# Attention layers' ends: scores between tiles, transposes by pairs, a norm of four chunks

## The chip, the cores and the metric

One core of a Trainium2 chip runs the whole program in one launch. The metric is device microseconds of that core, the median of several runs; a smaller number is better.

## The reference, cut to what matters

The program is a chain of seven stages on a sequence of 256 rows of width 1024: a gated feed-forward, a mixing stage, a second gated feed-forward, and then the second block, on which the change bears. That block has two layers, each an attention followed by a feed-forward with squared ReLU, and after each half a layer norm:

```
h = x * (1.0 + scale1) + shift1
y = moba_attention(h, ...)   # layer 0: 16 heads of 64, causal softmax
y = diff_attention(h, ...)   # layer 1: 8 heads, softmax(q1 k1) - lam * softmax(q2 k2)
x = layer_norm(ALPHA * x + (1.0 + gate1) * y, g, b)
h = x * (1.0 + scale2) + shift2
y = sq_relu_mlp(h, ...)
x = layer_norm(ALPHA * x + (1.0 + gate2) * y, g, b)
```

With 256 rows MoBA's only block is its own, so its attention is plain causal attention. In diff_attention each head's output also passes an RMS norm over its 128 columns. Both end in a product with a 1024x1024 output matrix.

## The kernel before, in words

Five engines run programs of their own, written out in order and tied by semaphores: SP loads weights, ACT and DVE split them and do the elementwise work, PE multiplies, POOL loads small tables. Each engine takes its instructions strictly in this written order, so the place of a wait matters as much as the wait.

**Weights.** Every product is made in fp32 accuracy from three products: hi x hi, hi x lo, lo x hi (`three`, L449 to L451). A unit is 128x2048 weights (1 MB) in one of six ring slots. ACT writes its high part (`split_hi`, L913), DVE the low part (`split_lo`, L1263), four units ahead of PE (`AHEAD`). An attention layer has 16 units: 0 to 11 are q, k and v (six blocks of two units), 12 to 15 the output matrix. For one unit PE makes 24 matmuls of 512 columns: two tiles t (128 rows each) x four chunks k x three products. Units 12 and 13 take chunks 0 to 3 of the attention's output, units 14 and 15 chunks 4 to 7. Unit 12 and 14 make columns 0 to 511 of the result, 13 and 15 the rest.

**A chunk of attention.** There are eight chunks c of 128 columns (two heads in MoBA, one head with two softmaxes in the other). For each, five steps pass between the engines; the table `ATTENTION` sets in which slot (behind which unit, or between its tiles) PE issues each:
- S: PE makes scores in banks 0 and 1 (`scores`, L809, L811), DVE scales, masks and finds the maxima (`scores` of DVE, L1778), ACT the exponentials (`exps`, L1194). In the second layer DVE then mixes the two softmaxes (`combine`, L1789 to L1795).
- W: PE transposes the weights into bank 2 (`weights_T`, L826), ACT copies them (`weights_out`, L1183).
- O: PE multiplies with v (`outputs`, L838 to L841) into the second half of bank 3. DVE divides by the sums (L1824, L1826); in the second layer ACT first takes squares (`squares`, L1204), and DVE multiplies by the gain (L1814) and later by the norm's factor (`norms`, L1804, then ten small steps in L1292 to L1301, then L1808).
- T: PE transposes finished output chunks (`outputs_T`, L559), ACT writes their high part (`chunk_his`, L920), DVE the low part (`chunk_los`, L1272). These feed units 12 to 15.
- H (L559, L1766): transposes of q and k heads, once per half.

ACT and DVE walk the same table and do the work of a slot's events one slot later. `probs` (the scores and exponentials of a chunk) is one buffer, `top` too; `total` has two. So scores(c) on DVE waits for the transposes of chunk c-1. In the table of before, T0 stands for all four chunks 0 to 3 behind unit 11, and T1 for chunks 4 to 7 behind O7; behind unit 13 come S7, O5, W6, O6, W7, O7 and T1 with no unit between them. In the second layer the norm is taken over chunks 0 to 2, then 3, then 4 to 6, then 7.

**The layer's end.** The layer norm (`after_ln`) works on four quarters of the result (tile t, half n): DVE adds the residual and takes statistics (`ln_part`, L1367 to L1370), for tile 0 both halves, then some nine small steps, then ACT normalises (L944), PE transposes (L523), ACT and DVE scale and split (L936, L1283, L1284), and the feed-forward's first unit can start.

Of the kernel before, what the change touches and what calls it, by code (L numbers as in the profile page):

```python
# [98 lines left out]
def quarter_buffer(b, t, h):  # L99
# [9 lines left out]

ATTENTION = [(0, [], []), (1, [], []), (2, [], []), (3, [], ["H0"]), (4, [], ["H1"]), (5, [], ["S0"]),  # L110
# [32 lines left out]
def two_blocks_kernel(nc, d, out):  # L143
    with ExitStack() as ctx:
# [50 lines left out]
        top = sb("top", [P, 2, NT])  # L195
        total = sb("total", [P, 2, 4])
# [9 lines left out]
        def part(off, n, t=None):  # L206
# [31 lines left out]
        probs = part(10240, 768)  # L238
        probs_w = part(11008, 384)
        rope2_t = [part(11392 + 128 * i, 128, NT) for i in range(4)]  # L240
        probsT = part(11904, 768)
        causal = part(12672, 3 * P)
        rot2 = part(13056, 4 * 8 * ROT).rearrange("p (c t n) -> p c t n", c=2, t=NT)
# [48 lines left out]
            sem(n) for n in ("rel_zero", "rel_in", "rel_out", "bias_in", "bias_done"))  # L292
        at_s, at_m, at_e, at_w, at_t, at_p, at_sq, at_o, at_out = (
# [152 lines left out]
        def _(pe):  # L446
# [345 lines left out]
            def attention(s, u0, pb, hb, ab, ch_o, diff):  # L792
# [22 lines left out]
                def weights_T(c):  # L815
# [5 lines left out]
                    if c % 4 == 0:  # L821
                        pe.wait_ge(at_out, ab + c)
                    src, n = (probs_w, 3) if diff else (probs, 6)
# [5 lines left out]
                def outputs(c):  # L829
# [3 lines left out]
                    n_e, width = (1, 2 * HD) if diff else (2, HD)  # L833
                    for e in range(n_e):
# [10 lines left out]
                def outputs_T(half):  # L845
                    pe.wait_ge(at_out, ab + 4 * half + 4)
                    if half == 0:
# [3 lines left out]
                    chunks_of(o2, half * BANK, 4, 4 * BANK if half == 0 else 0)  # L851
# [11 lines left out]

                entry(u0, s, zt if diff else x)
                do = {"H": heads_T, "S": scores, "W": weights_T, "O": outputs, "T": outputs_T}
                for slot, between, events in ATTENTION:
                    if slot is not None and 3 <= slot < 12:
                        if not between:
                            proj(u0, pb, slot // 2, slot % 2)
                        else:  # L870
# [1159 lines left out]
```

## Time and profile before

| | |
|---|---|
| median of 3 runs | 1284.71 us (1284.48 to 1284.99) |
| profiled execution | 1284.9 us, span 1283.1 us |
| PE busy | 1230.5 us (96%), 5777 matmuls |
| DVE, ACT, POOL busy | 931.4 (73%), 609.5 (48%), 95.7 us (7%) |
| MoBA layer's unit 11 to the first matmul of the feed-forward behind it | 706.82 to 762.33 us |
| the same of the second layer | 1027.15 to 1087.71 us |

The profiled execution's own time is 1.8 us over its span. The span runs from the first to the last instruction, all positions below are counted from its start. PE's rows carry modelled ends: a matmul of 512 columns starts 0.23 us after the one before it and is shown with 0.39 us. PEclk is the granted TensorE clock, 1.00 for 2.4 GHz and 0.50 for 1.2 GHz.

### The profile page before, as it was taken

The page shows a single profiled execution, that of the slowest core. Times are in us where ns is not written, and L with a number is a line of the kernel's source. Part 1 is how long each engine was busy: PE and PEld are TensorE (multiplying, and loading weights), DVE is VectorE, ACT ScalarE, POOL GpSimd, SP SyncE. Part 2 cuts the span into 40 slices and gives each one's busy share as a digit, 9 for nine tenths or more (in the row PEclk, how much of TensorE's full clock was granted, in tenths as well). Part 3 has the DMA queues.
Part 4 walks back from the last instruction along what each step waited for, and adds up shares of the span by engine and source line. Part 5 has one row for each costly group of instructions (what it writes and reads, how often), then busy time and mean ns, then how long its engine had stood idle before and what let it go on. Part 6 is the DMA issues. An engine that isn't in the chain of part 4 may idle for free.

```text
span 1283.1 us, 14651 instructions
## 1 busy us (share of the span) xinstructions
PE 1230.5 (96%) x5777; PEld 1010.8 (79%) x5777; DVE 931.4 (73%) x1349; ACT 609.5 (48%) x801; POOL 95.7 (7%) x136
## 2 busy tenths in 40 slices
PE   7999999999999999999999989999999986999996
PEld 6888887888888878888788768888877764888885
DVE  6789868865556698888775458896878776755446
ACT  6344446545664454443555535443455552634340
POOL 2100221003400010000000000000000000000000
PEclk9999999999999999999999979999999997999998
DMA  9999985544454598997473436798635441465530
GB/s 301 336 327 325 315 266 205 171 158 156 156 165 166 179 348 317 308 311 256 142 259 119 132 131 233 259 328 283 257 132 197 182 131 66 160 206 208 194 133 33
DMA packets 132916, 274.31 MB, mean 214 GB/s; under 512 B 6240, under 2 KB 51504, under 8 KB 132848
## 3 DMA queue, kind: packets, MB, share of 16 engines
q1 hardware_dynamic: 114992, 209.80, 47.6%
q0 software_dynamic: 17792, 63.56, 14.4%
q8 instruction: 46, 0.75, 0.2%
q14 instruction: 22, 0.18, 0.0%
q10 hardware_dynamic: 64, 0.02, 0.0%
HBM read 270.41 MB, written 2.93 MB: 213 GB/s over the span
## 4 chain that ended last, share of the span: by engine, by line
PE 87%; DVE 8%; ACT 2%; issue 2%; DMA 1%; ACTq 0%; DVEq 0%
PE ps L449 26%; PE ps L451 26%; PE ps L450 26%; PE ps L559 3%; DVE lo_w L1263 2%; ACT hi_w L913 1%; DMA w_raw<-in_diff_w_in 1%; PE ps L523 1%; PE ps L699 1%; PE ps L826 1%; PE ps L686 1%; PE ps L723 1%; PE ps L811 0%; PE ps L809 0%; PE ps L838 0%
## 5 line engine op out<-in xcount | busy, mean ns | idle before, releaser
L1263 DVE TENSOR_TENSOR lo_w<-w_raw,hi_w 128x2048 fp32r<-128x2048 f32 x197 | 447.3, 2290 | 99.1 <-ACT hi_w L913 98.9
L449 PE MATMUL ps<-hi_w,xT_hi 128*128 128x512 f32 x1120 | 449.7, 402 | 11.9 <-DVE xT_lo L1284 7.4
L451 PE MATMUL ps<-lo_w,xT_hi 128*128 128x512 f32 x1120 | 440.3, 393 | 0.0
L450 PE MATMUL ps<-hi_w,xT_lo 128*128 128x512 f32 x1120 | 439.6, 393 | 0.0
L913 ACT ACTIVATE hi_w<-w_raw 128x2048 fp32r<-128x2048 f32 x197 | 372.9, 1916 | 43.6 <-DMA w_raw<-in_w_mix_out 11.8
L449 PEld LDWEIGHTS ps<-hi_w,xT_hi 128*128 128x128 f32 x1120 | 212.8, 190 | 59.5 <-issue 15.7
L451 PEld LDWEIGHTS ps<-lo_w,xT_hi 128*128 128x128 f32 x1120 | 212.4, 190 | 46.0
L450 PEld LDWEIGHTS ps<-hi_w,xT_lo 128*128 128x128 f32 x1120 | 212.8, 190 | 42.0
L449 PE MATMUL ps<-hi_w,hT_hi 128*128 128x512 f32 x464 | 181.9, 392 | 0.4 <-DVE hT_lo L1426 0.4
L451 PE MATMUL ps<-lo_w,hT_hi 128*128 128x512 f32 x464 | 180.7, 389 | 0.0
L450 PE MATMUL ps<-hi_w,hT_lo 128*128 128x512 f32 x464 | 180.5, 389 | 0.0
L1426 DVE TENSOR_TENSOR hT_lo<-ps,hT_hi 128x512 fp32r<-128x512 f32 (+1 forms) x38 | 34.7, 914 | 93.6 <-ACT hT_hi L1046 67.4
L449 PEld LDWEIGHTS ps<-hi_w,hT_hi 128*128 128x128 f32 x464 | 87.1, 188 | 18.6 <-DVE hT_lo L1426 0.9
L451 PEld LDWEIGHTS ps<-lo_w,hT_hi 128*128 128x128 f32 x464 | 87.1, 188 | 18.2
L450 PEld LDWEIGHTS ps<-hi_w,hT_lo 128*128 128x128 f32 x464 | 87.2, 188 | 17.8
L1442 DVE SCALAR_TENSOR_TENSOR piece_acc<-aux,c_act,piece_acc 128x512 f32<-128x512 f32 x119 | 89.3, 751 | 3.6
L1046 ACT ACTIVATE hT_hi<-ps 128x1024 fp32r<-128x1024 f32 x16 | 16.4, 1027 | 131.4 <-PE ps L559 131.4
L1009 ACT ACTIVATE hT_hi<-ps 128x512 fp32r<-128x512 f32 x22 | 13.2, 598 | 114.0 <-PE ps L559 114.0
L559 PE MATMUL ps<-ident,area 128*128 128x128 f32 x384 | 53.5, 279 | 11.1 <-DVE area L1808 7.7
L559 PEld LDWEIGHTS ps<-ident,area 128*128 128x128 f32 x384 | 46.2, 143 | 20.6 <-DVE area L1808 8.4
L1001 ACT ACTIVATE area<-ps,rstd_x 128x256 f32<-128x256 f32 x44 | 18.5, 472 | 57.5 <-PE ps L451 57.5
L1902 POOL DMA_DIRECT2D aux<-in_ada_w x34 | 25.6, 753 | 234.4 <-DVE piece_acc L1442 213.4
(221 smaller groups left out, 887.9 us busy)
## 6 DMA issues: line engine op xcount, KB each, us to landing
w_raw<-in_ffn_w_in SPq DMA_DIRECT2D x86, 512.0 KB
aux<-in_ada_w POOLq DMA_DIRECT2D x34, 1024.0 KB, 6.4
w_raw<-in_mlp_w_up SPq DMA_DIRECT2D x32, 1024.0 KB
w_raw<-in_mlp_w_down SPq DMA_DIRECT2D x32, 1024.0 KB
w_raw<-in_w_mix_in SPq DMA_DIRECT2D x26, 1024.0 KB
w_raw<-in_ffn_w_out SPq DMA_DIRECT2D x22, 1024.0 KB
area<-in_ada_w POOLq DMA_DIRECT2D x14, 1024.0 KB, 7.5
w_raw<-in_moba_w_in SPq DMA_DIRECT2D x12, 1024.0 KB
```

The source lines that it names most:

```text
L449: pe.matmul(dst, lhs_hi, rhs_hi, start=start, stop=False)
L450: pe.matmul(dst, lhs_lo, rhs_hi, start=False, stop=False)
L451: return pe.matmul(dst, lhs_hi, rhs_lo, start=False, stop=stop)
L559: mm = pe.transpose(ps[:, off:off + P], src[:, t, col0 + c * P:col0 + (c + 1) * P], ident[:, :])
L913: act.activation(hi_w[:, ring_slot(u), :], w_raw[:, ring_slot(u), :], ACT.Copy).then_inc(w_hi, 1)
L1001: ins = act.activation(act_s[:, t, 0:FF_B], ps[:, (pair + t) * BANK:(pair + t) * BANK + FF_B], ACT.Silu, scale=rstd_x[:, t:t + 1])
L1009: act.activation(hi[:, c0:c0 + 2, :], ps[:, off:off + 2 * SEQ].rearrange("p (c n) -> p c n", c=2), ACT.Copy).then_inc(hidT_hi, 1)
L1046: act.activation(hi[:, c0:c0 + 4, :], bank(pair, 2).rearrange("p (c n) -> p c n", c=4), ACT.Copy).then_inc(hidT_hi, 1)
L1263: vec.tensor_tensor(lo_w[:, ring_slot(u), :], w_raw[:, ring_slot(u), :], hi_w[:, ring_slot(u), :].bitcast(F32), ALU.subtract).then_inc(w_l ...
L1426: vec.tensor_tensor(lo[:, c0:c0 + chunks, :], src.rearrange("p (c n) -> p c n", c=chunks), hi[:, c0:c0 + chunks, :].bitcast(F32), ALU.subt ...
L1442: ins = vec.scalar_tensor_tensor(out=acc, in0=row, scalar=c_act[:, c:c + 1], in1=acc, op0=ALU.mult, op1=ALU.add)
L1902: pool.dma_start(dst, ada[layer][:, 4 * half:4 * half + 4, i * BANK:(i + 1) * BANK])\
```

## The change

The table is rewritten from unit 11 on, and slot 13 differs by layer:

```diff
-             (9, ["H2"], ["O2", "W3"]), (10, ["H3"], ["S4", "O3"]), (11, [], ["T0", "S5", "W4"]),
-             (12, [], ["S6", "O4", "W5"]), (13, [], ["S7", "O5", "W6"]), (None, [], ["O6", "W7"]),
-             (None, [], ["O7"]), (None, [], ["T1"]), (14, [], []), (15, [], [])]
+             (9, ["H2"], ["O2", "W3"]), (10, ["H3"], ["S4", "O3"]), (11, ["S5", "T0"], ["T1", "W4"]),
+             (12, ["S6"], ["O4", "W5"])]
+MOBA_SLOTS = ATTENTION + [(13, ["S7", "O5", "W6"], ["O6"]), (14, [], [])]
+DIFF_SLOTS = ATTENTION + [(13, ["S7"], ["O5", "W6", "O6"]), (14, [], [])]
+PAIR_BANK, NORMED = (4, 5, 0, 1), (1, 2, 3, 3)
```

The middle list of a slot is issued between the unit's two tiles. T0 to T3 are now pairs of chunks, each in a bank of its own. `probs` and `top` have two buffers, `total` four:

```diff
-        probs = part(10240, 768)
-        probs_w = part(11008, 384)
+        probs = [part(10240, 768), part(11008, 768)]
+        moba_probsT = part(11776, 768)
+        probs_w, diff_probsT = part(11776, 384), part(12160, 384)
...
-                    if c % 4 == 0:
+                    if c % 4 == 0 or c == 7 and not diff:
                         pe.wait_ge(at_out, ab + c)
...
+                        if not diff:
+                            outputs_T(2)
+                        weights_T(7)
+                        outputs(7)
+                        if diff:
+                            outputs_T(2)
+                            outputs_T(3)
+                        pe.wait_ge(w_lo, u0 + 15)
+                        last_quarter(0, 0, 0)
+                        if not diff:
+                            outputs_T(3)
+                        pe.wait_ge(w_lo, u0 + 16)
+                        last_quarter(1, 0, 0)
+                        last_quarter(0, 0, 2).then_inc(part_done, 1)
+                        last_quarter(1, 0, 2).then_inc(part_done, 1)
```

`last_quarter(n, t, c)` makes the six matmuls of unit 14+n, tile t, for two chunks; for tile 0 it takes chunks 4 and 5 of both units first, then 6 and 7 of both. Tile 1 follows as before. On DVE:

```diff
                     vec.wait_ge(at_s, ab + c + 1)
-                    vec.wait_ge(at_e, ab + c)
-                    if diff:
-                        vec.wait_ge(at_w, c)
-                    else:
-                        vec.wait_ge(at_t, ab + c)
+                    if c >= 1:
+                        vec.wait_ge(at_e, ab + c - 1)
+                    if diff and c >= 2:
+                        vec.wait_ge(at_w, c - 1)
+                    elif not diff and c >= 2:
+                        vec.wait_ge(at_t, ab + c - 1)
...
-                        if c % 4 < 3:
+                        if c % 4 < 3 and c < 6:
                             vec.wait_ge(at_p, ab + c + 2)
...
+                    if diff and slot == 10:
+                        norms(0, 2)
+                    if diff and slot == 11:
+                        norms(2, 2)
...
+                if diff:
+                    outputs(5)
+                    combine(7)
+                    outputs(6)
+                    outputs(7)
+                    norms(4, 4)
+                    pair_los(2)
+                else:
+                    outputs(6)
+                    pair_los(2)
+                    outputs(7)
+                pair_los(3)
+                split_lo(u0 + 18)
```

and on ACT, behind the last slot:

```diff
+                if diff:
+                    squares(6)
+                    weights_out(7)
+                    squares(7)
+                    pair_his(2)
+                else:
+                    pair_his(2)
+                    weights_out(7)
+                pair_his(3)
+                split_hi(u0 + 18)
```

Before, `split_hi(u0 + 18)` and `split_lo(u0 + 18)` stood behind O6's work and ahead of chunk 7's. The exponentials' wait is now for the chunk four back.

PE at the end of the MoBA layer before, from O7 to unit 14's first matmuls (L838 to L841 are O7, L559 is T1, L449 to L451 unit 14):

```order
L838 MATMUL ps<-area 128x64 [waits proj_out,at_outputs_out,at_weightsT_out]
L839 MATMUL ps<-area 128x64
L841 MATMUL ps<-area 128x64
...
L559 MATMUL ps<-ident,area 128x128 [waits at_max,at_outputs_out]
L559 MATMUL ps<-ident,area 128x128 x7
L449 MATMUL ps<-hi_w,xT_hi 128x512 [waits ch_lo,w_lo]
```

and now, from behind O6 (L564 are the pairs T2 and T3, L831 is W7, L844 starts O7, L454 unit 14 and then unit 15):

```order
L564 MATMUL ps<-ident,area 128x128 [waits at_max,at_outputs_out]
L564 MATMUL ps<-ident,area 128x128 x3
L831 MATMUL ps<-ident,area 128x128 [waits at_outputs_out,at_weightsT_out,at_exp]
L831 MATMUL ps<-ident,area 128x128 x5
L844 MATMUL ps<-area 128x64 [waits proj_out,at_outputs_out,at_weightsT_out]
...
L454 MATMUL ps<-hi_w,xT_hi 128x512 [waits ch_lo,w_lo]
...
L564 MATMUL ps<-ident,area 128x128 [waits at_max,at_outputs_out]
L564 MATMUL ps<-ident,area 128x128 x3
L454 MATMUL ps<-hi_w,xT_hi 128x512 [waits ch_lo,w_lo]
```

T2 has moved ahead of W7, and T3 stands between the first six matmuls of unit 14 and those of unit 15.

DVE at the same place before (L1824 and L1826 are outputs 6, then 7; L1263 splits unit 18; L1272 is the low part of chunks 4 to 7; L1367 opens the layer norm):

```order
L1824 RECIPROCAL inv<-total 128x4 [waits at_weightsT_out,at_outputs]
L1826 TENSOR_TENSOR area<-ps,inv 128x2x2x64 [waits vec_step]
L1263 TENSOR_TENSOR lo_w<-w_raw,hi_w 128x2048 [waits w_hi]
L1824 RECIPROCAL inv<-total 128x4 [waits at_outputs]
L1826 TENSOR_TENSOR area<-ps,inv 128x2x2x64 [waits vec_step]
L1272 TENSOR_TENSOR xT_lo<-ps,xT_hi 128x256 [waits ch_act] x4
L1367 TENSOR_TENSOR area<-ps,aux 128x512 [waits ld_row,part_done]
```

and now (L1886 and L1888 outputs, L1334 low parts by pairs, L1325 the split, L1429 the layer norm):

```order
L1886 RECIPROCAL inv<-total 128x4 [waits at_outputs]
L1888 TENSOR_TENSOR area<-ps,inv 128x2x2x64 [waits vec_step]
L1334 TENSOR_TENSOR xT_lo<-ps,xT_hi 128x256 [waits ch_act] x2
L1886 RECIPROCAL inv<-total 128x4 [waits at_outputs]
L1888 TENSOR_TENSOR area<-ps,inv 128x2x2x64 [waits vec_step]
L1334 TENSOR_TENSOR xT_lo<-ps,xT_hi 128x256 [waits ch_act] x2
L1325 TENSOR_TENSOR lo_w<-w_raw,hi_w 128x2048 [waits w_hi]
L1429 TENSOR_TENSOR area<-ps,aux 128x512 [waits ld_row,part_done]
```

The split of unit 18 has moved from ahead of outputs 7 to a place right ahead of the layer norm, and outputs 6 no longer waits for the copy of W7 (at_weightsT_out).

DVE in the second layer, around unit 12's start before (L1795 ends combine(4), L1263 splits unit 15, L1272 is the low part of chunks 0 to 3, L1778 scores 5):

```order
L1795 SCALAR_TENSOR_TENSOR area<-area,inv 128x256
L1263 TENSOR_TENSOR lo_w<-w_raw,hi_w 128x2048 [waits w_hi]
L1272 TENSOR_TENSOR xT_lo<-ps,xT_hi 128x256 [waits ch_act] x4
L1778 ISA area,top<-ps,area 128x128 [waits at_weights,at_exp,at_scores]
```

and now (L1334 low parts, L1852 to L1858 combine(4), L1841 scores 5, L1325 the split):

```order
L1334 TENSOR_TENSOR xT_lo<-ps,xT_hi 128x256 [waits ch_act] x2
L1852 SCALAR_TENSOR_TENSOR head_eps<-total 128x2 [waits at_weightsT,at_exp]
...
L1858 SCALAR_TENSOR_TENSOR area<-area,inv 128x256
L1841 ISA area,top<-ps,area 128x128 [waits at_weights,at_exp,at_scores]
...
L1325 TENSOR_TENSOR lo_w<-w_raw,hi_w 128x2048 [waits w_hi]
L1334 TENSOR_TENSOR xT_lo<-ps,xT_hi 128x256 [waits ch_act] x2
```

The first pair of low parts comes ahead of combine, scores and the split, the second pair behind all three.

## Rows read from the trace of the kernel before

**Rows 1.** PE's waits, 620 to 765 us: line <- releaser: us in total, times, longest.

```profile
PE ps L449 <- DVE xT_lo L1284: 2.9, 2, 2.2
PE ps L838 <- issue: 2.0, 1, 2.0
PE ps L838 <- ACT area L1183: 1.7, 1, 1.7
PE ps L559 <- DVE area L1826: 1.1, 1, 1.1
PE ps L826 <- ACT area L1194: 0.7, 1, 0.7
PE ps L449 <- DVE xT_lo L1272: 0.4, 1, 0.4
```

**Rows 2.** The same, 930 to 1095 us.

```profile
PE ps L559 <- DVE area L1808: 7.7, 2, 6.8
PE ps L838 <- issue: 3.2, 2, 1.6
PE ps L449 <- DVE xT_lo L1272: 2.8, 2, 2.3
PE ps L826 <- DVE area L1795: 1.6, 1, 1.6
```

**Rows 3.** Windows of PE: stretch, length, busy (instructions), PEclk, DMA share, GB/s.

```profile
706.82:762.33 55.51, 47.20 (x243) 0.88 0.30 105
1027.15:1087.71 60.56, 43.05 (x208) 0.86 0.29 97
1040.00:1042.00 2.00, 2.00 (x6) 0.50 0.00 0
978.00:982.00 4.00, 2.51 (x12) 1.00 0.19 51
```

**Rows 4.** The chain of waits in order of time: start, us, what.

```profile
748.28 0.43 PE ps L450
...
770.77 0.23 PE ps L450
...
1060.49 0.63 ACT aux L1204 x4
```

**Rows 5.** ACT's groups, 700 to 765 us: busy us, mean ns | idle before.

```profile
L913 ACT ACTIVATE hi_w<-w_raw 128x2048 fp32r<-128x2048 f32 x5 | 9.5, 1901 | 0.0
...
L1183 ACT ACTIVATE area<-ps 128x768 f32<-128x768 f32 x4 | 3.2, 812 | 8.3 <-PE ps L826 8.3
...
L920 ACT ACTIVATE xT_hi<-ps 128x256 fp32r<-128x256 f32 x8 | 2.5, 384 | 6.8 <-PE ps L559 6.8
```

**Rows 6.** DVE's groups, the same stretch.

```profile
L1263 DVE TENSOR_TENSOR lo_w<-w_raw,hi_w 128x2048 fp32r<-128x2048 f32 x5 | 11.4, 2290 | 11.5 <-ACT hi_w L913 11.5
L1778 DVE CUSTOM_DVE_ANT_0 area<-ps,area 128x256 f32<-128x256 f32 x8 | 3.4, 420 | 0.0
...
L1826 DVE TENSOR_TENSOR area<-ps,inv 128x256 f32<-128x256 f32 x5 | 2.1, 424 | 0.2
```

**Rows 7.** DVE's timeline: start, us, instruction.

```profile
750.86 0.69 DVE L1367 TENSOR_TENSOR area<-ps,aux 128x512 f32<-128x512 f32 x1 [3.58 <-PE ps L451]
...
753.58 0.69 DVE L1367 TENSOR_TENSOR area<-ps,aux 128x512 f32<-128x512 f32 x1 [0.57 <-PE ps L451]
...
757.72 0.16 DVE L1382 SCALAR_TENSOR_TENSOR shift<-moments,rstd 128x1 f32<-128x1 f32 x1
...
1051.18 0.75 DVE L1795 SCALAR_TENSOR_TENSOR area<-area,inv 128x128 f32<-128x128 f32 x2
...
1061.60 0.17 DVE L1804 TENSOR_TENSOR head_sq<-head_sq,head_eps 128x6 f32<-128x6 f32 x1
...
1063.82 0.96 DVE L1808 TENSOR_TENSOR area<-area,head_rstd 128x768 f32<-128x768 f32 x1
...
1069.65 0.43 DVE L1808 TENSOR_TENSOR area<-area,head_rstd 128x256 f32<-128x256 f32 x1
```

More of the change, by code:

```diff
@@ L850, in outputs_T @@
                         pe.wait_ge(at_m, ab + 8)
-                    chunks_of(o2, half * BANK, 4, 4 * BANK if half == 0 else 0)
+                    chunks_of(o2, 2 * pair * P, 2, PAIR_BANK[pair] * BANK)
                 def modulation_rows():
@@ L862, in modulation_rows_2, with last_quarter @@
                         .then_inc(mod_T, 1)
+                def last_quarter(n, t, c):
+                    u = u0 + 14 + n
+                    rhi = hi_w[:, ring_slot(u), :].rearrange("p (k n) -> p k n", k=4)
+                    rlo = lo_w[:, ring_slot(u), :].rearrange("p (k n) -> p k n", k=4)
+                    for k in range(c, c + 2):
+                        if t == 0:
+                            pe.wait_ge(ch_lo, ch_o + 4 + k + 1)
+                        mm = three(bank(4 + n + 2 * t), xT_hi[:, 4 + k, tile(t)], xT_lo[:, 4 + k, tile(t)],
+                                   rhi[:, k, :], rlo[:, k, :], False, k == 3)
+                    return mm
@@ L1840, in attention @@
                             scores(int(event[1:]))
+                    for event in last_between:
+                        if event[0] == "S" and diff:
+                            combine(int(event[1:]))
                     for event in before:
@@ L1853, in attention @@
                             combine(int(event[1:]))
-                    if diff and ("O2" in before or "O6" in before):
-                        c = 2 if "O2" in before else 6
-                        vec.wait_ge(at_out, ab + c + 1)
-                        then(norms(c - 2, 3))
-                    if slot is not None and slot < 14:
-                        split_lo(u0 + slot + AHEAD)
+                    for event in between:
+                        if event[0] == "S":
+                            scores(int(event[1:]))
+                    split_lo(u0 + slot + AHEAD)
                     if slot == 2 and diff:
@@ L1864, in attention @@
                         second_modulation()
-                    if "O7" in events:
-                        split_lo(u0 + 18)
-                    before = events
+                    for event in between:
+                        if event[0] == "O":
+                            outputs(int(event[1:]))
+                    before, last_between = events, between
+                if diff:
+                    outputs(5)
[4 more added lines that the diff above has]
+                    pair_los(2)
+                else:
+                    outputs(6)
[3 more added lines that the diff above has]
+                split_lo(u0 + 18)
             attention(U_MOBA, PB_MOBA, 4, NA_H, CH_MOBA_O, False)
```

157 lines of the change are left out of this document (90 added, 67 removed).

## The prediction

> **What bounds the kernel now.** The page first: PE is busy 96% of the span, so only PE's holes and the stretches in which its clock is low can be won. The edits bear on the last units of the two attention layers, so I read PE's waits there. In the MoBA layer they are short and many [rows 1]: 2.0 us of "issue" at an outputs step (O6), 0.7 at W7, 1.7 at O7, 1.1 at T1, 0.4 at unit 14, and 2.2 at the feed-forward's first unit. With 0.2 that the first tile of unit 12 waits, the stretch from unit 11 to the feed-forward has 8.4 us of shown holes. In the second layer [rows 2] it is 6.8 behind DVE's norm at T1 and 0.9 at T0, 2.3 and 0.5 at units 12 and 14, 3.2 at O6 and O7, 1.6 at W7, and again 2.2 at the feed-forward: 17.5 us. The windows of both stretches [rows 3] give their lengths, 55.5 and 60.6 us, and that the granted clock was 0.88 and 0.86 there. A matmul at the lower level, 1.2 GHz, goes on after 0.43 us and one at 2.4 GHz after 0.23 [rows 4], so each costs 0.20 more.
>
> From this comes what PE must work in each stretch. A hole as shown leaves out the modelled tail of the matmul before it, about 0.2 to 0.25 us (0.39 shown, 0.23 to the next); seven such holes are 1.7 us in the MoBA layer, eight are 2.0 in the other. Clock: in the MoBA layer I count W7, O7, T1 and some eight matmuls of unit 14 at the lower level, 4.3 us lost; in the second layer seven matmuls of unit 12 (the window at 1040 is at 0.50 [rows 3]), O7, T1 and two or three of unit 14, 3.4 us. Work at full clock is then 55.5 - 8.4 - 1.7 - 4.3 = 41.1 us, and 60.6 - 17.5 - 2.0 - 3.4 = 37.7 us. The change alters no PE work (120 large matmuls, three scores, four weights and outputs, the sixteen transposes of T stay), so what counts is the new holes. I count these whole, with their tails.
>
> **The change, part by part: MoBA layer.** Scores between the tiles: S5, S6 and S7 are 2.7 us (twelve matmuls of 0.23) earlier, and the exponentials with them. O6 now stands behind tile 1 of unit 13 and finds outputs 5 and the copy of W6 ready: its 2.0 us hole goes. At W7 PE now waits for outputs 6: O6's tail of 0.2 and the two steps of DVE (0.2, and 0.42 for L1826 [rows 6]), of which T2's four transposes, about half a us, hide most: 0.4 us. O7 waits for W7's copy: 0.81 [rows 5] and tail and handshake of 0.35, 1.2 us; nothing hides it, and it is cheaper than before only because outputs 6 no longer follows that copy. T2's high and low parts are done by then. T3 waits for outputs 7, made beneath the six matmuls of unit 14 (1.4 us), and its copies lie under the six of unit 15: no hole. The second pair at unit 12 is late by 0.2 us, since DVE splits unit 15 ahead of it. Unit 12's first tile no longer waits for the last projection.
>
> Then the end pays. Take T3's first transpose as zero. ACT's copy is done at 1.4 (0.7 for the four transposes, 0.7 for two L920 of 384 ns, less overlap), and only then splits unit 18's high part, 1.90 us [rows 5], and DVE the low part, 2.29 [rows 6]: DVE is free at about 5.5. All of it stood earlier before. The first quarter of the layer norm is ready on PE at 3.5, so it starts 2.0 us late. From 753.58 to the shift's end at 757.88 is 4.3 us, and the quarter ahead of it takes 2.2 (750.86 to the statistics' end, [rows 7]): 12.0. With 0.8 for ACT's normalising the transposes can start at 12.9. PE has its own work done at 10.3 (0.5 of transposes, then 6 + 12 + 24 matmuls). Hole: 2.5 us, where there was 0.1. Interleaving the units by chunks makes it worse: quarter (0, 0) comes only 1.4 us ahead of (0, 1), and DVE needs 2.2 for it, so of the 2.5 about 0.8 would stand without the split. With 0.3 between the two transposes and 2.3 to the first unit as before, the holes are 0.2 + 0.4 + 1.2 + 2.5 + 0.3 + 2.3 = 6.9 us, plus 0.4 for the clock at these transposes. After: 41.1 + 6.9 + 0.4 = 48.4 against 55.5: 7.1 us less. Neither hole at W7 or O7 should drop the clock: 1.5 us in one piece at 980 left it at 1.00 [rows 3].
>
> **Second layer.** DVE is the tight engine. norms(2, 2) stands ahead of combine(4): ten small steps and L1804 take 2.2 us whatever the width (1061.60 to 1063.82), and the multiply 0.96 for 768 columns and 0.43 for 256 [rows 7], so about 0.7 for 512. Scores 4 end after norms(0, 2) and a split, which leaves 0.6 at S5, and combine(4), 1.3 us (0.75 for its last two steps at 1051.18 [rows 7], 0.5 for the three small ones), another 0.6 at W4. From the first pair's low part DVE goes on to combine, scores (four passes of 0.42 or less [rows 6], 1.2 together), the split of 2.3 and only then the second pair, 0.3: 5.0 us. PE has 0.2 left, T1, the 0.6, W4 and six matmuls, 3.0: hole 2.0. So here 3.2 us replace the 3.2 of before, nothing is won, and 1.5 us of lower clock behind them stays.
>
> Behind unit 13 S7 and combine(7) are ahead of time. O6 waits for W6's copy, 1.1; W7 for combine(7), 0.5; O7 for a copy of 0.5, 0.85 in all. T2 waits for the squares, 0.63 [rows 4], L1814, 0.4, and one norm of four chunks, 2.2 + 1.2 = 3.45: with the tail 4.9 us. Before, the same point was 6.8 late since norm 4 to 6, the split of unit 18 (2.3) and a second norm of 2.6 stood in line. The first of unit 14 waits 1.0 for copy and low part. Here T2 and T3 come together ahead of all 48 matmuls, so the split of unit 18 is over in time and only the interleaving costs: 0.65. Sum: 0.6 + 0.6 + 2.0 + 1.1 + 0.5 + 0.85 + 4.9 + 1.0 + 0.65 + 0.3 + 2.3 = 14.8 us. Clock: 1.5 at unit 12, 1.1 at T2, T3 and unit 14, 0.3 at the end: 2.9. After: 37.7 + 14.8 + 2.9 = 55.4 against 60.6: 5.2 us less.
>
> Costs I put at nothing: two score buffers in slots 5 to 10, since PE has no hole there but those at the head transposes; moved areas; the wait of W7 for outputs 6 beyond what is counted. The last split hides behind the layer norm in one layer only. The feed-forward starts behind the same 2.2 us hole as before, so it keeps the same stretch at 1.2 GHz. Weight loads are no closer: their DMA share in both stretches is 0.3 [rows 3]. Each hole rests on one handshake that I know to 0.1 us, and there are seventeen; together with the clock, known to 1.5 us a layer, the sum of 12.3 us lies between 9 and 16.
>
> **Sum.** 1284.9 (the profiled execution) - 12.3 = 1272.6; the median of the runs shown is 0.2 lower, so 1272.4 us.
>
> **The rivals.**
> First: DVE in the second layer. Between units 10 and 13 it gets a norm, both splits, combine and scores in one line with PE waiting behind each; if any is later than I count, units 12 and 13 wait for it and the holes move rather than close. For it speaks that PE's longest waits there are all on DVE [rows 2]; against it that DVE's work is unchanged in sum, one norm less. It would win 2 instead of 5.2 in this layer: 1275.6.
>
> Second: the clock takes back part in the MoBA layer. Holes of 0.4 and 1.2 us stand 0.6 us apart, the ones at the end make 5.1 in 6 us. If the first pair brings it down, some 9 us at 1.2 GHz follow, ten to fifteen matmuls at 0.20 and the small steps: 2.5 us, 1274.9. Against: 980 us, above. The other way, if the 2.0 us hole at unit 12 of the second layer leaves the clock up, 1.5 more is won: 1270.9.
>
> Third, and this one ends slower: PE's many short holes hold the clock at 1.2 GHz from unit 12 to the end of both layers. Before, one long pause let PE run 40 to 48 matmuls in a piece at 2.4 GHz; now every group is cut. 96 large matmuls per layer at 0.20 are 19 us; for half of them in each layer, 19 us in all, the result is 1272.4 + 19 = 1291. It decides from about 60 matmuls at the lower level on (12.3 / 0.20). Against it: between the new holes stand 3 to 6 us of unbroken work. The Trainium skill states such a rule (TensorE: Matmul & The Clock Gate, section "A second HAM failure mode: psum-queue depth-cycling"): a kernel whose PE pauses shortly and often between groups of matmuls swung between both clock levels and lost throughput. By that rule this change, which spreads PE's groups, would come out at 1291; the trace has it only behind holes of 2 us and more.
>
> Fourth: the change does not do what it says, since each step still waits for the one before and only the place of the wait moves. Then both layers stay within 2 us of before: 1283.
>
> **How the numbers follow.** Forecast 0.62, with its own range 1269 to 1276; DVE's line 0.14 and the clock in the MoBA layer 0.13; held clock 0.03; nothing gained 0.04; anything else slower 0.01, anything else faster 0.03. The range that leaves two in ten out goes to 1268.5 below (the clock stays up at unit 12 and some holes are shorter) and to 1278 above (both first rivals together, with a part of the unknown). About 0.2%, 2.6 us, is what can be told from no change. Faster 0.92, same 0.04, slower 0.04.
>
> **What would show it.** In the profile after: no hole of over 0.3 us between unit 11 and O6 in the MoBA layer; 1.2 us at O7; the layer norm's first step right behind the split of unit 18 and a hole of 2 to 3 us ahead of the first transposes of the feed-forward, against under 1 in the second layer; there 4 to 6 us ahead of T2, behind a single norm of eight columns, and about 2 us within unit 12's first tile. Wrong would be: PEclk near 0.5 over unit 13 of the MoBA layer, a hole of over 3 us on weights, or an S step that waits for DVE by over 1 us.

## The result, and the profile after

The changed kernel takes 1269.8 us (median of 4 runs, 1269.74 to 1271.83) against 1284.6 before: a ratio of 0.9891 (0.9879 to 0.9903), 14.8 us less. Forecast were 1272.4 us, 12.3 less. The profiled execution has a span of 1268.0 us (before 1283.1) and a mean granted clock of 0.99 (before 0.982).

The two stretches that the change touches, as windows of the trace after; the columns are those of [rows 3]:

```profile
706.24:754.82 48.58, 43.13 (x243) 0.97 0.40 137
1019.52:1072.78 53.26, 41.44 (x208) 0.93 0.34 115
```

By the places of these windows the 15.1 us of span come from: the MoBA stretch 6.9 (55.51 to 48.58), the second layer's 7.3 (60.56 to 53.26), and 0.9 from the three parts around them (0.6, 0.1 and 0.2). Both clocks rose, from 0.88 to 0.97 and from 0.86 to 0.93.

PE's waits, 625 to 1095 us, answer to [rows 1] and [rows 2] together (us in total, times, longest):

```profile
PE ps L454 <- DVE xT_lo L1346: 5.8, 4, 2.2
PE ps L564 <- issue: 4.7, 1, 4.7
PE ps L528 <- ACT area L977: 4.5, 4, 2.3
PE ps L844 <- ACT area L1217: 2.4, 3, 0.9
PE ps L454 <- DVE xT_lo L1334: 2.1, 2, 1.7
...
PE ps L831 <- DVE area L1858: 0.5, 2, 0.3
PE ps L831 <- DVE area L1888: 0.4, 1, 0.4
PE ps L814 <- DVE top L1841: 0.3, 1, 0.3
```

The 2.0 us at O6 of the MoBA layer is gone, the 1.7 us at its O7 is down to 0.9, the three of 1.6 us in the second layer are down to 0.9, 0.2 and 0.6, and the 6.8 us behind DVE's norm to 4.7. The greatest that remain are this 4.7 us, one of 2.3 ahead of the MoBA layer's feed-forward transposes, the feed-forwards' own 2.2, and 1.7 at unit 12. Where each stands, in PE's timeline of the MoBA layer (start, us, instruction, idle time before it and its releaser):

```profile
733.96 0.85 PE L831 MATMUL ps<-ident,area 128*128 128x128 f32 x6 [0.38 <-DVE area L1888]
...
735.71 0.43 PE L844 MATMUL ps<-area 128*128 128x64 f32 x2 [0.90 <-ACT area L1217]
...
751.12 1.82 PE L528 MATMUL ps<-ident,area 128*128 128x128 f32 x8 [2.30 <-ACT area L977]
...
754.82 0.77 PE L454 MATMUL ps<-hi_w,xT_hi 128*128 128x512 f32 x1 [1.88 <-DVE xT_lo L1346]
```

and of the second layer:

```profile
1027.80 0.55 PE L831 MATMUL ps<-ident,area 128*128 128x128 f32 x3 [0.30 <-DVE area L1858]
...
1031.44 0.50 PE L454 MATMUL ps<-hi_w,xT_hi 128*128 128x512 f32 x1 [1.70 <-DVE xT_lo L1334]
...
1046.39 0.46 PE L844 MATMUL ps<-area 128*128 128x128 f32 x2 [0.89 <-ACT area L1217]
1047.53 0.55 PE L831 MATMUL ps<-ident,area 128*128 128x128 f32 x3 [0.23 <-DVE area L1858]
1048.65 0.49 PE L844 MATMUL ps<-area 128*128 128x128 f32 x2 [0.58 <-ACT area L1217]
1054.29 1.94 PE L564 MATMUL ps<-ident,area 128*128 128x128 f32 x8 [4.70 <-issue]
1056.68 0.77 PE L454 MATMUL ps<-hi_w,xT_hi 128*128 128x512 f32 x1 [0.45 <-DVE xT_lo L1334]
...
1069.24 1.36 PE L528 MATMUL ps<-ident,area 128*128 128x128 f32 x8 [0.49 <-ACT area L977]
1072.78 0.77 PE L454 MATMUL ps<-hi_w,xT_hi 128*128 128x512 f32 x1 [2.17 <-DVE xT_lo L1346]
```

DVE's timeline answers to [rows 7]. First the MoBA layer's end, then the second layer between the two low parts ahead of unit 12, then the norm of four chunks ahead of T2:

```profile
741.67 2.29 DVE L1325 TENSOR_TENSOR lo_w<-w_raw,hi_w 128x2048 fp32r<-128x2048 f32 x1 [1.04 <-ACT hi_w L946]
743.88 0.68 DVE L1429 TENSOR_TENSOR area<-ps,aux 128x512 f32<-128x512 f32 x1
...
1025.81 0.75 DVE L1334 TENSOR_TENSOR xT_lo<-ps,xT_hi 128x256 fp32r<-128x256 f32 x2
...
1028.77 2.29 DVE L1325 TENSOR_TENSOR lo_w<-w_raw,hi_w 128x2048 fp32r<-128x2048 f32 x1
1030.97 0.75 DVE L1334 TENSOR_TENSOR xT_lo<-ps,xT_hi 128x256 fp32r<-128x256 f32 x2
...
1050.74 0.17 DVE L1869 TENSOR_TENSOR head_sq<-head_sq,head_eps 128x8 f32<-128x8 f32 x1
...
1052.96 1.23 DVE L1873 TENSOR_TENSOR area<-area,head_rstd 128x1024 f32<-128x1024 f32 x1
```

The layer norm (L1429) starts in the very moment in which the split of unit 18 ends. The second low part ahead of unit 12 comes 5.16 us behind the first (forecast 5.0), behind combine, scores and a split. The norm is one line of 3.45 us (forecast 3.45), 1050.74 to 1054.19, and T2 follows at 1054.29.

The clock, in PE's windows after; [rows 3] had 0.50 at unit 12 of the second layer:

```profile
752.00:754.00 2.00, 0.94 (x4) 0.50 0.95 307
1030.00:1032.00 2.00, 0.56 (x2) 1.00 0.80 310
1032.00:1034.00 2.00, 2.00 (x14) 1.00 0.00 0
1052.00:1054.00 2.00, 0.00 (x0) 0.50 0.00 0
```

Behind the 1.70 us hole the clock now stays up. Read in such windows from 20 us to PE's last matmul, the time at 1.2 GHz fell from 37.5 us to 17.0 (behind that matmul, where PE has nothing left to do, both traces have one more low stretch up to their end): before 13.6 us from 736 on, 3.4 from 762, 3.4 from 1038, 13.7 from 1060 and 3.4 from 1086; after 6.8 from 750, 6.8 from 1050 and 3.4 from 1072.

### The profile page after: what moved, and what is told of

It is laid out like the page before. It is cut to its first block, busy times and chain, and to the rows that moved or that the text cites. A ratio compares the mean times of both kernels' runs of the same rounds, so it can differ in the third digit from the quotient of the medians.

```text
span 1268.0 us, 14635 instructions
## 1 busy us (share of the span) xinstructions
PE 1223.2 (96%) x5777; PEld 1003.9 (79%) x5777; DVE 928.9 (73%) x1337; ACT 609.2 (48%) x801; POOL 95.2 (8%) x136
## 4 chain that ended last, share of the span: by engine, by line
PE 83%; DVE 8%; ACT 3%; DMA 3%; issue 2%; SPq 1%; DVEq 0%; ACTq 0%
PE ps L454 25%; PE ps L456 25%; PE ps L455 25%; PE ps L564 3%; DVE lo_w L1325 2%; ACT hi_w L946 1%; DMA w_raw<-in_ffn_w_out 1%; DMA w_raw<-in_diff_w_in 1%; DMA w_raw<-in_ffn_w_in 1%; PE ps L528 1%; PE ps L704 1%; PE ps L831 1%; DVE area L1430 1%; DVE bst L1432 1%; DVE area L1429 1%
## 5 line engine op out<-in xcount | busy, mean ns | idle before, releaser
L1325 DVE TENSOR_TENSOR lo_w<-w_raw,hi_w 128x2048 fp32r<-128x2048 f32 x197 | 447.5, 2290 | 86.5 <-ACT hi_w L946 86.0
L454 PE MATMUL ps<-hi_w,xT_hi 128*128 128x512 f32 x1120 | 449.1, 401 | 10.3 <-DVE xT_lo L1346 7.1
L454 PEld LDWEIGHTS ps<-hi_w,xT_hi 128*128 128x128 f32 x1120 | 211.5, 189 | 59.0 <-issue 13.2
L454 PE MATMUL ps<-hi_w,hT_hi 128*128 128x512 f32 x464 | 182.0, 392 | 0.5 <-DVE hT_lo L1488 0.5
L454 PEld LDWEIGHTS ps<-hi_w,hT_hi 128*128 128x128 f32 x464 | 87.1, 188 | 18.7 <-DVE hT_lo L1488 0.9
L1042 ACT ACTIVATE hT_hi<-ps 128x512 fp32r<-128x512 f32 x22 | 13.1, 597 | 112.5 <-PE ps L564 112.5
L564 PE MATMUL ps<-ident,area 128*128 128x128 f32 x384 | 53.2, 277 | 7.8 <-issue 4.7
L564 PEld LDWEIGHTS ps<-ident,area 128*128 128x128 f32 x384 | 45.6, 142 | 17.8 <-issue 5.5
```

The source lines that it names most:

```text
L454: pe.matmul(dst, lhs_hi, rhs_hi, start=start, stop=False)
L564: mm = pe.transpose(ps[:, off:off + P], src[:, t, col0 + c * P:col0 + (c + 1) * P], ident[:, :])
L1042: act.activation(hi[:, c0:c0 + 2, :], ps[:, off:off + 2 * SEQ].rearrange("p (c n) -> p c n", c=2), ACT.Copy).then_inc(hidT_hi, 1)
L1325: vec.tensor_tensor(lo_w[:, ring_slot(u), :], w_raw[:, ring_slot(u), :], hi_w[:, ring_slot(u), :].bitcast(F32), ALU.subtract).then_inc(w_l ...
```

## The experiments

The main theory: the holes close as forecast, each for its own reason, and what the sum missed is clock. The rivals: DVE's line in the second layer, clock taken back in the MoBA layer, and a gain that comes from somewhere else, such as the buffers.

**Each layer alone.** A copy of before's program of an attention layer stands beside the new one, for one layer.

```diff
-            attention(U_DIFF, PB_DIFF, 8, NA_H + 8, CH_DIFF_O, True)
+            attention_old(U_DIFF, PB_DIFF, 8, NA_H + 8, CH_DIFF_O, True)
```

> The new order and the new waits in the MoBA layer alone; the second layer keeps the old table, norms and end. Theory (the gain is the sum of holes closed in each layer, and the layers don't touch each other): the stretch from unit 11 to the feed-forward is 48.6 us in the MoBA layer and 60.6 in the second, 7 us off the whole: 1277.6. Rival (part of the gain of one layer is lost or made in the other, by loads or by the clock): this run and the one with the second layer alone don't add up to 14.8 within 1 us.

Measured: 1278.9 us (1277.9 to 1279.3), ratio 0.9957 (0.9940 to 0.9973), 5.6 us less. The stretch in the MoBA layer is 48.4 us (expected 48.6). The hole ahead of the feed-forward's transposes is 2.33 us, and in the second layer both great holes of before stand: 2.33 us at unit 12 and 6.84 at T1.

> The new order in the second layer alone. Theory: 55.5 us in the MoBA layer and 53.3 in the second, 7.3 us off the whole: 1277.3; PEclk stays at 1.00 through units 12 and 13 of the second layer. Rival (the clock stayed up there only because the whole program had moved against it): the clock falls within unit 12 as before, and 5.8 us are won, as I had predicted for this layer with its clock: 1278.8.

Measured: 1277.0 us (1276.3 to 1277.5), ratio 0.9942 (0.9927 to 0.9957), 7.5 us less. Unit 12's hole is 1.71, T2's 4.70, as in the whole change. So the second layer brought 7.5 alone, not 5.2: here is the miss. By their medians the two layers alone make 13.1 us, together 14.8; that meets the rival's condition (more than 1 us apart), but the intervals of these gains are about 2 us to either side, so the medians don't decide it. The profiled executions do: the two stretches are 7.1 and 7.0 us shorter where each layer stands alone, 14.1 in sum, and 14.2 in the whole change. What differs lies outside them. Unit 11 of the MoBA layer starts anywhere from 705.87 to 706.95 us in the fourteen traces, with no order by kernel. And the part between the stretches takes 265.6 us in the run with the MoBA layer alone, 264.7 in the changed kernel: the low stretch of 6.8 us begins 1.9 us behind the end of the 2.33 us hole in the one and 0.35 us behind it in the other, so that 5.2 and 3.5 us of it fall on the feed-forward's matmuls.

**Only the buffers.** Before's order with the new, doubled areas.

```diff
-        top = sb("top", [P, 2, NT])
-        total = sb("total", [P, 2, 4])
+        top = sb("top", [P, 2, 2, NT])
+        total = sb("total", [P, 4, 4])
...
-        probs = part(10240, 768)
+        probs = [part(10240, 768), part(11008, 768)]
```

> The kernel before with one part of the change alone: two buffers for probs and top, four for total, and the waits that go with them (scores and exponentials); table, order, transposes, norms and the split of unit 18 are as before. Theory (the order closed the holes, the buffers only allow it): exponentials 7 of the MoBA layer still stand behind the copy of W6 on ACT, outputs 5 still waits for that copy; O6's hole shrinks by 0.5 and W7's start moves by 1.4 us, the second layer gains nothing: 1283.1. Rival (the buffers are the gain): 1280 or less.

Measured: 1283.3 us (10 runs, 1282.7 to 1284.3), ratio 0.9992 (0.9982 to 1.0001). The interval takes in 1, so this is not told apart from no change. In the MoBA layer the hole at W7 goes, and the one at O6 is 1.69 us instead of 2.0, as the waits show:

```profile
PE ps L838 <- ACT area L1183: 3.4, 2, 1.7
```

The buffers alone bring some 1 us (0 to 2.3 by the interval); the order that they allow brings the rest. This run's clock shows one thing more. The hole at O6 is the only one of over 0.3 us within the 30 us before it, and the clock falls about 1 us behind its end (PE's timeline, then a window of PE):

```profile
733.61 0.41 PE L838 MATMUL ps<-area 128*128 128x64 f32 x2 [1.69 <-ACT area L1183]
...
734.00:736.00 2.00, 2.00 (x14) 0.63 0.00 0
```

So a hole of 1.69 us brought the clock down here, between matmuls of 64 columns and transposes, while one of 1.70 us at unit 12 of the changed kernel, followed by matmuls of 512 columns, did not.

**Unit 12's hole and the clock.** In the changed kernel one idle addition on DVE makes this hole as long as before.

```diff
+                    if diff and "T1" in before:
+                        for _ in range(1):
+                            vec.tensor_tensor(aux[:, 3072:3584], aux[:, 3072:3584], aux[:, 3072:3584], ALU.add)
```

> The changed kernel with one more DVE instruction of 0.7 us (an addition on scratch that nothing reads) ahead of the second pair's low part in the second layer: the hole within unit 12's first tile grows from 1.7 to 2.4 us, as long as the 2.3 us hole ahead of unit 12 was before. Theory (1.7 us is too short to bring the clock down, 2.3 is enough; that is the 1.5 us by which my sum for this layer was too high): PEclk falls to 0.50 for some 3.4 us within units 12 and 13, and the time grows by 2.4 us, 1272.2. Rival (before, it fell for the 0.9 and 2.3 us holes together, not for one of 2.3): PEclk stays at 1.00 and 0.7 us are lost, 1270.5.

Measured: 1272.5 us (1271.3 to 1274.3), ratio 0.9905 (0.9891 to 0.9920). PE's timeline at the hole:

```profile
1032.09 0.79 PE L454 MATMUL ps<-hi_w,xT_hi 128*128 128x512 f32 x1 [2.31 <-DVE xT_lo L1334]
```

The window that begins there (columns as in [rows 3]):

```profile
1032.00:1034.00 2.00, 1.91 (x5) 0.50 0.00 0
```

PE starts 5 large matmuls in 1.91 us, some 0.43 apart, where one at 2.4 GHz goes on after 0.23 [rows 4]. For 0.6 us more of hole the median is 2.7 us later (1.8 by the ratios); 3.4 us at half clock account for up to 1.7 of it. That clock is what the forecast had kept and the change did away with. The two intervals of the ratio overlap, so the size is less sure than the clock, which the window shows. The other traces agree at this place: the clock fell in all four with a hole of 2.31 to 2.33 us here (`before`, `buffers_only`, `moba_only`, `hole_at_12`) and stayed up in all five with one of 1.70 to 1.72 (`after`, `after_again`, `second_only`, `split_early`, `norm_3_1`). It is no length that holds elsewhere, as `buffers_only` shows.

**The norm of four chunks.** Three chunks and then one, the split of unit 18 still out of the way.

```diff
-PAIR_BANK, NORMED = (4, 5, 0, 1), (1, 2, 3, 3)
+PAIR_BANK, NORMED = (4, 5, 0, 1), (1, 2, 4, 4)
...
+                    norms(4, 3)
...
-                    norms(4, 4)
+                    norms(7, 1)
```

> The changed kernel with the second layer's last norm in two parts again: chunks 4 to 6 behind outputs 6, chunk 7 behind outputs 7; T2 and T3 wait for both. Theory (the hole ahead of T2 fell from 6.8 to 4.7 us because the split of unit 18, 2.3, no longer stands in that line; three chunks' norm runs while PE and ACT still make chunk 7): the hole is 5.1 us, the time 0.4 longer, 1270.2. Rival (the one norm of four chunks brought it): the hole is 6.5 us or more and the time 2 us longer.

Measured: 1270.9 us (1270.7 to 1272.2), ratio 0.9895 (0.9879 to 0.9912). T2's hole:

```profile
1054.96 1.94 PE L564 MATMUL ps<-ident,area 128*128 128x128 f32 x8 [5.11 <-issue]
```

So one norm instead of two brings 0.4 us of the 2.1 by which this hole shrank (6.8 to 4.7). The other 1.7 are put down to the split of unit 18, which no longer stands between two norms; that is argued from the rows, since no run has the split alone back at that place. From O7's start to the transposes it is 8.46 us before (1061.67 to 1070.13), 6.05 here and 5.64 in the changed kernel, and the 2.4 us between the first two are close to the 2.3 us of the split. DVE's timeline of this run shows why the single norm brings so little: the first norm, the gain of chunk 7 (L1879) and the second norm.

```profile
1048.71 0.17 DVE L1869 TENSOR_TENSOR head_sq<-head_sq,head_eps 128x6 f32<-128x6 f32 x1
...
1051.80 0.42 DVE L1879 TENSOR_TENSOR area<-ps,subln 128x256 f32<-128x256 f32 x1
...
1054.43 0.43 DVE L1873 TENSOR_TENSOR area<-area,head_rstd 128x256 f32<-128x256 f32 x1
```

In the changed kernel L1879 starts 1.63 us behind O7 (1050.28 and 1048.65); here, with O7 at 1048.91, it could at 1050.54 and is held up 1.26 us by the first norm. The second norm then takes 2.60 us instead of 3.45, which gives 0.85 back.

**The split of unit 18 at its old place in the MoBA layer** (ACT's part likewise).

```diff
+                    split_lo(u0 + 18)
...
-                split_lo(u0 + 18)
+                if diff:
+                    split_lo(u0 + 18)
```

> The changed kernel with one edit in the MoBA layer: unit 18 is split behind outputs 7 and ahead of the high and low parts of T3, instead of right ahead of the layer norm. Theory (the 2.3 us hole ahead of the feed-forward's transposes is the split on DVE, 2.0 of it, and the interleaved quarters): the hole goes to 0.6 us, the layer norm's first step follows the low parts at once, the whole is 1.7 us shorter: 1268.1. Rival (the interleaving of the quarters by itself, or ACT, makes the hole): it stays at 2 us or more, and the time is the same within 0.5 us.

Measured: 1267.9 us (1267.5 to 1269.2), ratio 0.9874 (0.9859 to 0.9888):

```profile
749.47 1.36 PE L528 MATMUL ps<-ident,area 128*128 128x128 f32 x8 [0.49 <-ACT area L977]
```

The hole falls from 2.30 to 0.49, and the feed-forward starts at 753.01 instead of 754.82. The forecast had put the split's part at 1.7 of 2.5 us; it is 1.8. In this execution the low stretch at the MoBA layer's feed-forward is 3.4 us instead of 6.8, and the one at the second layer's 6.8 instead of 3.4.

**The low part of unit 15 behind the second pair**, in the second layer, so that unit 12 needn't wait for it.

```diff
+                            if diff and event == "T1":
+                                split_lo(u0 + 11 + AHEAD)
...
-                    split_lo(u0 + slot + AHEAD)
+                    if not (diff and slot == 11):
+                        split_lo(u0 + slot + AHEAD)
```

> The changed kernel with one edit in the second layer: DVE splits unit 15 behind the low part of the second pair, no longer ahead of it. Theory (the 1.7 us hole within unit 12's first tile is that split standing in line): the hole goes, 1.7 us off the whole, 1268.1, no matter what the clock does, since it was up before. Rival (the pair's transposes or ACT's copy are late as well, or the split is late for unit 15 instead): under 0.7 us won.

Measured: 1270.0 us (1269.7 to 1270.3), ratio 0.9888 (0.9874 to 0.9903): nothing, and the expectation was wrong. The hole at unit 12 is gone, and the feed-forward starts 1.1 us earlier:

```profile
1071.65 0.77 PE L454 MATMUL ps<-hi_w,xT_hi 128*128 128x512 f32 x1 [2.17 <-DVE xT_lo L1346]
```

Its windows there tell what took it back:

```profile
1066.00:1076.00 10.00, 7.29 (x26) 0.74 0.58 207
1076.00:1086.00 10.00, 10.00 (x46) 0.92 0.01 2
```

The same windows of the changed kernel:

```profile
1066.00:1076.00 10.00, 7.29 (x29) 0.83 0.58 210
1076.00:1086.00 10.00, 10.00 (x49) 1.00 0.01 2
```

The low stretch that begins about 1070 lasts 6.8 us instead of 3.4, and PE makes six matmuls fewer in these 20 us. The edit is not needed for that: `split_early`, whose second layer is that of the changed kernel, has the same 6.8 us from 1070. The second layer's own stretch, from unit 11 to the feed-forward, is 51.0 us in place of 53.3, so 2.3 us were won there in this execution. Against them stand 1.4 us behind the feed-forward's start, where the clock was low longer, and 1.3 us in parts ahead of the edit: 0.65 before the MoBA layer's unit 11 and 0.65 between the stretches, which differ as much between executions of other kernels.

**All of it together, and PE kept busy.** `best` has both edits and in the second layer unit 14's first tile whole ahead of unit 15's. `warm` adds matmuls with no use, whose results nobody reads: 19 ahead of T2, 9 behind the feed-forward's first transposes of both layers and one ahead of them in MoBA. `warm_starts` is `warm` without the 19.

```diff
+                def keep(n):
+                    for _ in range(n):
+                        pe.matmul(bank(2), hT_hi[:, 0, 0:P], hT_hi[:, 0:2, :].rearrange("p c n -> p (c n)"),
+                                  start=True, stop=True)
...
+                            keep(19)
...
+                        keep(0 if diff else 1)
...
+                        keep(9)
```

> The changed kernel with three edits: unit 18 split behind outputs 7 in the MoBA layer (as in split_early), unit 15's low part behind the second pair's in the second layer (as in lo15_behind), and in the second layer unit 14's tile 0 whole ahead of unit 15's, so that the quarters of the layer norm come 2.7 us apart. Theory: the hole of 2.3 goes to 0.5, the one of 1.7 to 0.3, the one of 0.5 ahead of the last feed-forward's transposes to 0.1; 3.6 us less, 1266.2. Stretches at 1.2 GHz of 3.4 us, each worth 1.7 us, may come or go at both feed-forward starts: 1264.5 to 1267.9. Rival (the clock takes back what the holes give, as in lo15_behind): 1268 or more.

Measured: 1266.8 us (1266.5 to 1267.3), ratio 0.9860 (0.9846 to 0.9875). That is 0.6 us from the 1266.2 of the theory and inside its range. The low stretches of the profiled execution are 6.8 us from 752, 10.2 from 1046 and 3.4 from 1070.

> The kernel of the run best with PE kept at work in its longest holes: 19 matmuls of 512 columns, whose result nobody reads, ahead of T2 in the second layer (4.7 us), one ahead of and nine behind each layer's last transposes (2.2 us). They add no wait and end before the work behind them could start. Theory (what is left of the clock's loss comes from these holes: 6.8, 10.2 and 3.4 us at 1.2 GHz in best, of which PE worked some 11): PEclk stays at 1.00 through both layers, 5 us less than best, 1261.8. Rival (the added matmuls stand in the way or the clock falls for another reason, its own timing): within 1.5 us of best, 1265.3 or more.

Measured: 1263.7 us (1263.1 to 1264.5), ratio 0.9838 (0.9821 to 0.9854), the fastest kernel of the study, 6.1 us below the changed one and 3.1 below `best`, of the 5 expected. Its PE timeline in the second layer:

```profile
1042.15 0.46 PE L849 MATMUL ps<-area 128*128 128x128 f32 x2 [0.89 <-ACT area L1230]
1043.29 0.55 PE L836 MATMUL ps<-ident,area 128*128 128x128 f32 x3 [0.23 <-DVE area L1873]
1044.41 0.62 PE L849 MATMUL ps<-area 128*128 128x128 f32 x2 [0.58 <-ACT area L1230]
1045.55 5.76 PE L801 MATMUL ps<-hT_hi 128*128 128x512 f32 x19
...
1053.04 0.47 PE L454 MATMUL ps<-hi_w,xT_hi 128*128 128x512 f32 x1 [0.86 <-DVE xT_lo L1349]
```

The 4.7 us hole is filled, and unit 14 runs at 2.4 GHz from its start. One low stretch of 3.4 us is left, from 1044 on, behind the three short holes. It makes the 19 matmuls last 5.76 us, longer than planned: the norm ends at 1050.49, and T2 starts only at 1051.14, where the changed kernel starts it 0.1 us behind the norm. So the added matmuls do stand in the way here, by some 0.5 us, which the expectation had ruled out.

> The same without the 19 matmuls ahead of T2: only the starts of the two feed-forwards are kept busy. Theory: the clock still falls within the 4.7 us hole and stays low over T2, T3 and the first matmuls of unit 14 (some 7 us, 1.5 lost), but no longer at the two starts, 1.6 to 3 us won each over best: 1263.3. Rival: the stretch at 1.2 GHz that begins in the second layer's tail reaches on whatever stands at the start, and only the MoBA layer's is won: 1265.

Measured: 1265.8 us (1265.2 to 1266.4), ratio 0.9855 (0.9841 to 0.9870). This gains 1.1 us on `best`, not 3.5. The median is nearer to the rival's, but not for its reason: PEclk stays up at both feed-forward starts, and the only low stretch is 6.8 us from 1050 on, behind T2's hole. In the profiled executions the first 96 large matmuls of the feed-forward take 24.8 us instead of 26.6 in the MoBA layer, but 24.8 instead of 25.3 in the second, where 1.6 to 3 us had been expected of each; in both a hole of 0.64 us has opened ahead of the next transposes. By the medians the fill at T2 is worth 2.1 us (the intervals of the two ratios overlap). Of the 1.7 us between the two profiled executions the second layer's stretch makes 0.8 (51.3 to 50.5), and another 0.8 lies ahead of unit 11 of the MoBA layer, where the two kernels are the same.

**Two kernels once more,** one profiled execution each, since one run of the changed kernel had taken 1271.83 us.

> The changed kernel unaltered, one more profile. Theory (the places at which the clock falls are given by the holes, but how long it stays down, 3.4, 6.8 or 10.2 us, differs from execution to execution): holes equal to the first profile's within 0.1 us, stretches at 1.2 GHz again behind T2's hole and at both feed-forward starts, at least one of them by 3.4 us longer or shorter. Rival (the kernel's order sets the lengths too): 6.8, 6.8 and 3.4 us again.

Measured: 1271.8 us. From W7 of the MoBA layer to the second feed-forward the holes of both layers' ends are the same to 0.04 us (but for the MoBA feed-forward's first matmul, 2.17 for 1.88); the clock is not. PE's timeline at W7 and O7 of the MoBA layer:

```profile
733.67 0.85 PE L831 MATMUL ps<-ident,area 128*128 128x128 f32 x6 [0.37 <-DVE area L1888]
...
735.42 0.43 PE L844 MATMUL ps<-area 128*128 128x64 f32 x2 [0.90 <-ACT area L1217]
```

PE's windows from there on:

```profile
734.00:736.00 2.00, 1.10 (x10) 1.00 1.01 394
736.00:738.00 2.00, 2.00 (x12) 0.66 0.06 22
738.00:740.00 2.00, 2.00 (x7) 0.50 0.00 0
```

In this execution a stretch of 3.4 us follows the two short holes, and the MoBA layer's stretch is 50.0 us instead of 48.6. In the second layer a stretch of 10.2 us replaces the one of 6.8, and it begins earlier: the window 1050 to 1052 is at 0.67 though T2's hole opens only at 1051.46, so it begins behind the three short holes at O6, W7 and O7, not in T2's. (`best` is alike: 0.52 in 1046 to 1048, T2's hole opens at 1047.90.) The loss behind W7 and O7 of the MoBA layer is the second rival: of the eleven traces with these two holes it is in two, `after_again` and `best_again`, and costs 1.4 us in each.

> The kernel of best unaltered, one more profile. Theory: as above, the lengths 6.8, 10.2 and 3.4 us don't all come again. Rival: they do, and 10.2 is this order's price for its short holes at W7 and O7 of the second layer.

Measured: 1267.9 us, with the same 3.4 us from 736 on, and 6.8 at 1050 where the first execution had 10.2 at 1046. As the theory said, the lengths did not all come again.

## Why the prediction was right, and where it was off

The mechanism was the one forecast, and its range (1268.5 to 1278.0) holds the time. The sum was 2.5 us short of the gain. By its own steps, holes counted whole as the sum counts them, the shown hole plus about 0.2 us of tail:

| step | forecast | after |
|---|---|---|
| MoBA: W7, O7 | 0.4, 1.2 | 0.6, 1.1 |
| MoBA: transposes, first unit | 2.5, 2.3 | 2.5, 2.1 |
| second layer: S5, W4, unit 12 | 0.6, 0.6, 2.0 | 0.5, 0.5, 1.9 |
| O6, W7, O7 | 1.1, 0.5, 0.85 | 1.1, 0.45, 0.8 |
| T2, first of unit 14 | 4.9, 1.0 | 4.9, 0.65 |
| transposes, first unit | 0.65, 2.3 | 0.7, 2.4 |

**MoBA stretch:** forecast 48.4 us, measured 48.6. (The shown holes of before add up to 8.3 us, where the text has 8.4; nothing hangs on it.) S5 to S7 between the tiles, O6 without a wait, T3 hidden and the late layer norm all came as said, and there is no hole between unit 11 and O6. `split_early` shows that the 2.5 us at the end have the cause that the text named, and how much of it is the split. One sentence failed, and its cost was hidden by luck: "it keeps the same stretch at 1.2 GHz". With the new hole ahead of the transposes it is 6.8 us at this feed-forward, not 3.4. (Without that hole it was 3.4 in `split_early` but 6.8 in `best`, so the hole is not shown to be the only cause.) In the profiled execution 3.5 us of it fall behind the first matmul, as 3.4 did before, and nothing is lost. In the five other traces with this hole 4.4 to 5.2 us do, which costs 0.5 to 0.9 us.

**Second layer:** forecast 55.4 us, measured 53.3. The step that failed is "nothing is won, and 1.5 us of lower clock behind them stays". The hole at unit 12 was sized right (1.9 whole, for 2.0); but the row of before that it replaces, 2.3 us [rows 2], is shown without its tail, 2.5 whole. The new hole was 0.6 shorter, not the same, and the clock followed: it stayed at 1.00 behind 1.70 us shown and fell behind 2.31 in `hole_at_12`. So the term "clock 2.9 us" should have been 1.4: by the sum, 53.3 less 37.7 of work and 14.2 of holes. (That is a remainder, and 37.7 is itself an estimate; what the windows show directly is that nothing is lost at unit 12, for which the sum had 1.5.) The other 0.6 is holes, more than half of it at unit 14's first matmul, which waited 0.65 us instead of 1.0. That the clock stays up here was the "other way" of the second rival, for which the text had 1.5 us.

**Outside the stretches** 0.9 us of span came that the sum had at nothing, 0.6 of it ahead of unit 11. That 0.6 is no gain of the change: unit 11 starts between 705.87 and 706.95 us in the fourteen traces, at 706.82 in that of before, and at 706.24 and 705.93 in the two of the changed kernel. `buffers_only`, with the old order, has 706.23. So a part of the 15.1 us between the two profiled executions is the spread of that start.

**The rivals.** DVE's line in the second layer (1275.6) did not decide: 5.16 us for 5.0. The clock in the MoBA layer (1274.9) left the profiled execution alone, and took part of the gain in others. "Does not do what it says" (1283) is refuted by both stretches, each some 7 us shorter; 1283 was roughly what the buffers alone do. The held clock (1291) is refuted as a loss of 19 us: PEclk is 0.97 and 0.93 over the two stretches. But the reason that the text gave against it, that the clock fell "only behind holes of 2 us and more", did not hold for the kernel before either: in its second layer the window 1060 to 1062 is at 0.57, behind holes of 1.60 and 1.63 us and within a third of 1.60, and T1's long one opens only at 1063.29. A small form of this rival exists: `warm` and `best` have a low stretch behind holes of 0.89, 0.23 and 0.58 us at 1044 to 1046, `after_again` one behind 0.37 and 0.90 at 736. The Trainium skill's section "A second HAM failure mode: psum-queue depth-cycling" (TensorE: Matmul & The Clock Gate) describes this: short, frequent pauses between groups that bring the clock down. The trace agrees that it can happen, for 3.4 us in `warm` and `after_again`, in some executions of a kernel and not in others.

## What to carry to other kernels

Count a hole in the same way before and after (with the tail of the matmul before it, or without), above all where the clock hangs on it: within unit 12, 1.7 us shown kept it and 2.3 lost it, and 0.6 us of hole was worth up to 1.7 more. Don't carry that length elsewhere: 1.69 us lost the clock at O6 in `buffers_only`, and 0.37 with 0.90 lost it in two of eleven traces. Where an operation is moved off one engine's queue past a waiting consumer, look who stands behind its new place; here a 2.3 us split was worth some 1.7 us at T2 when it left (argued, not run by itself) and cost 1.8 at the MoBA layer's end where it went. A pause that can't be closed can be filled with matmuls that nobody reads, but their count must hold at the low clock too, or they outlast the pause. A single edit of 1 us can vanish in the clock, so try such edits together, and compare stretches of the traces beside the medians.

## What the runs showed of the hardware that was not expected

- Stretches at 1.2 GHz came as 3.4, 6.8, 10.2 or 13.7 us in all fourteen traces (from 20 us to PE's last matmul, read in windows of 2 us), and in no other length. Behind the same two holes of the same instructions (0.49 and 2.17 us at the second feed-forward) it was 3.4 us in `after` and 6.8 in `split_early`; behind 0.49 and 2.17 at the MoBA layer's it was 3.4 in `split_early` and 6.8 in `best`. With PE busy throughout, 3.4 us more at 1.2 GHz cost 1.7 us, which is about the spread of the changed kernel's own runs (1269.74 to 1271.83).
- Where the low stretch begins moves too. In six traces with the 2.3 us hole ahead of the MoBA layer's feed-forward transposes it begins 0.35 to 1.9 us behind the hole's end.
- A start that comes 1.1 us earlier can meet a longer low stretch and win nothing (`lo15_behind`).
- The small dependent steps of DVE's norm start 0.20 us apart at two, six and eight columns, and take 0.17 us each: what they cost is their number.
